# State space scan: the decay matrix is built as exponent(sums spread by float32r plus a mask) on ScalarE

## What is computed

```python
z, xbc, dt = split_cols(h @ w_in, SSM_SPLITS)
xbc = silu(causal_conv4(xbc) + conv_b);  x, B, C = split(xbc)
dt = softplus(dt + dt_bias);  a = dt * -exp(a_log)
cum = cumsum(a)                                # along time, per head
seg = cum[..., :, None] - cum[..., None, :]    # [l, s]
L = exp(where(l >= s, seg, -inf))
y_diag = einsum(C @ B.T, L, x * dt)            # inside a chunk
y_off = C @ state * exp(cum)                   # from the chunk before
y = (y_diag + y_off + d_skip * x) * silu(z);  rmsnorm per group;  @ w_out
```

## Time and profile before

| | |
|---|---|
| median of 3 runs | 2073.43 us (2073.12 to 2076.48) |
| the profiled execution | 2075.21 us, of it the span of the trace 2073.4 us |
| PE busy, share of the span | 1975.6 us, 95% |
| DVE busy | 1725.3 us, 83% |
| ACT busy | 1328.1 us, 64% |
| DMA, mean share of 16 engines | 74% |
| granted TensorE clock, mean | 0.982 of full |
| state space layer's blocks and scan | about 442 to 700 us of the span |
| the scan's 40 steps | about 514 to 667 us |

### The profile page before, as it was taken

How to read it: one execution, slowest core, us unless ns; L and a number is a source line. 1 busy time by engine, 2 the same in 40 slices (tenths; PEclk the granted TensorE clock), 3 DMA queues, 4 the chain that set the end, 5 groups by cost and what they waited for, 6 DMA issues and landing times.

```text
span 2073.4 us, 28446 instructions
## 1 busy us (share of the span) xinstructions
PE 1975.6 (95%) x10316; PEld 1644.3 (79%) x10316; DVE 1725.3 (83%) x2440; ACT 1328.1 (64%) x1977; POOL 0.2 (0%) x4
## 2 busy tenths in 40 slices
PE   6998999989989999999999999999999998999997
PEld 5777889978877788788888878888888876767785
DVE  7798878768776698989989898998989988785764
ACT  4353534355564587788788787888878774554543
POOL 0000000000000000000000000000000000000000
PEclk9999999999999999999999999999999999999999
DMA  9856689846332298999999999999989994672630
GB/s 378 300 170 234 229 301 327 287 142 207 116 111 82 91 382 325 359 334 382 366 351 365 329 368 345 374 352 340 371 325 377 380 354 158 222 247 68 217 122 21
DMA packets 154211, 560.19 MB, mean 270 GB/s; under 512 B 17232, under 2 KB 17488, under 8 KB 153936
## 3 DMA queue, kind: packets, MB, share of 16 engines
q1 hardware_dynamic: 154064, 558.29, 74.1%
HBM read 557.18 MB, written 1.05 MB: 269 GB/s over the span
## 4 chain that ended last, share of the span: by engine, by line
PE 78%; DVE 12%; ACT 5%; issue 3%; DMA 2%; DVEq 0%; SPq 0%; ACTq 0%
PE ps L527 22%; PE ps L529 22%; PE ps L528 22%; PE ps L533 10%; DVE spl L516 3%; PE ps L537 3%; DVE macc L580 2%; ACT sph L504 2%; DMA ring<-in_hyb_w_in 1%; DVE arena L2169 1%; DMA ring<-in_dense_down 1%; ACT arena L771 1%; ACT arena L2135 0%; DVE hL L884 0%; ACT ps L890 0%
## 5 line engine op out<-in xcount | busy, mean ns | idle before, releaser
L504 ACT ACTIVATE sph<-ring 128x1024 fp32r<-128x1024 f32 x906 | 949.2, 1059 | 517.0 <-PE ps L529 332.8
L516 DVE TENSOR_TENSOR spl<-ring,sph 128x1024 fp32r<-128x1024 f32 x906 | 1078.2, 1219 | 241.5 <-ACT sph L504 229.0
L527 PE MATMUL ps<-sph,hH 128*128 128x512 f32 (+1 forms) x1296 | 522.6, 403 | 1.4 <-DVE hL L884 1.3
L529 PE MATMUL ps<-sph,hL 128*128 128x512 f32 (+1 forms) x1296 | 507.8, 392 | 0.0
L528 PE MATMUL ps<-spl,hH 128*128 128x512 f32 (+1 forms) x1296 | 506.9, 391 | 0.0
L529 PEld LDWEIGHTS ps<-sph,hL 128*128 128x128 f32 x1296 | 245.5, 189 | 52.6
L527 PEld LDWEIGHTS ps<-sph,hH 128*128 128x128 f32 x1296 | 246.4, 190 | 51.3 <-issue 3.8
L528 PEld LDWEIGHTS ps<-spl,hH 128*128 128x128 f32 x1296 | 246.4, 190 | 48.4 <-issue 1.0
L527 PE MATMUL ps<-sph,rH 128*128 128x512 f32 x664 | 269.1, 405 | 5.9 <-ACT arena L3123 2.3
L529 PE MATMUL ps<-sph,rL 128*128 128x512 f32 x664 | 259.9, 391 | 0.0
L528 PE MATMUL ps<-spl,rH 128*128 128x512 f32 x664 | 259.4, 391 | 0.0
(11 more groups left out here) (317 smaller groups left out, 1754.4 us busy)
## 6 DMA issues: line engine op xcount, KB each, us to landing
ring<-in_moe_gu SPq DMA_DIRECT2D x448, 512.0 KB, 5.4
ring<-in_moe_down SPq DMA_DIRECT2D x224, 512.0 KB, 5.3
ring<-in_mod SPq DMA_DIRECT2D x144, 512.0 KB, 5.0
ring<-in_w_in SPq DMA_DIRECT2D x64, 512.0 KB, 4.5
ring<-in_dense_gu SPq DMA_DIRECT2D x44, 512.0 KB, 5.3
ring<-in_ssm_w_in SPq DMA_DIRECT2D x40, 512.0 KB, 4.2
ring<-in_dense_down SPq DMA_DIRECT2D x22, 512.0 KB, 5.4
ring<-in_hyb_w_in SPq DMA_DIRECT2D x20, 512.0 KB, 5.9
```

The source lines that it names most:

```text
L504: a.activation(k.high[m % SPLITS][:, 0:w], raw[:, 0:w], ACT.Copy).then_inc(k.S.half_rounded, 1)
L516: v.tensor_tensor(k.low[m % SPLITS][:, 0:w], raw[:, 0:w], k.high[m % SPLITS][:, 0:w], ALU.subtract).then_inc(*k.tick(k.S.half_split, f"hal ...
L527: pe.matmul(out, a[0], b[0], start=start, stop=False, skip_group_check=True)
L529: return pe.matmul(out, a[1], b[0], start=False, stop=stop, skip_group_check=True)
```

## The change

- **The exponent moves and is cut.** At r = 0 and r = 1 ACT reads the bank itself: four exponents of 128 columns with the negated own sum as bias (`M.less`), 64 in all. The 64 DVE instructions at L2280 and the 8 exponents of 1024 columns at r = 2 are gone. Banks with sums are now freed by ACT (`raised{r}`); DVE's product at r = 3 waits for `raised1`.
- **The mask** is a product: the identity by a matrix `past` (0 on and above the diagonal of the stored matrix, -1e30 elsewhere), in float32r, 512 columns, opens each bank.
- **The sums** come from `cum`, turned once per time tile by PE, split into a high part (ACT) and a low part (DVE) in 64 rows of the old `dtw3` tile; a 0/1 column of `pick`, spread over 128 columns, picks both rows of a head. These products are float32r too, one per head, 128 columns.
- **Set up once**, in the dt part: four small DVE writes (zeros, `pick`, `eye`, `past`), the negated sums, the low part; one ACT copy; two transposes on PE.
- The arena grows, two tiles are added, and a scratch area for dynamic DMA is asked for at 1024 bytes.

```diff
@@ time_tensor
     yield
+    bank = banks.take(pe, "cumT", "dt.low")
+    pe.wait_ge(*when("dt.sums"))
+    for t in range(NT):
+        last = turn(pe, k, bank[0:32, t * 128:(t + 1) * 128], M.cum[:, t, :])
+    last.then_inc(*tick(S.dt_tensor, "dt.turned"))
+    yield
@@ time_scalar
+    a.wait_ge(*when("dt.turned"))
+    a.activation(M.cumT[0:32, :], k.banks[k.bank_of.get("cumT", 0)][0:32, 0:T], ACT.Copy).then_inc(*tick(S.dt_scalar, "dt.high"))
+    yield
@@ time_vector
     v.tensor_tensor(M.dte, M.dte, M.dtb[:, 0, :], ALU.mult).then_inc(*tick(S.dt_vector, "dt.weights"))
+    v.memset(M.cumT[64:128, :].bitcast(F32), 0.0).then_inc(*tick(S.dt_vector, "dt.low"))
+    v.tensor_copy(M.pick, k.caus_spare[:, 32:64]).then_inc(*tick(S.dt_vector, "dt.low"))
+    v.tensor_copy(M.eye, k.C["ident"]).then_inc(*tick(S.dt_vector, "dt.low"))
+    v.tensor_scalar(M.past, k.C["triu"], 1.0, -NEG, ALU.subtract, ALU.mult).then_inc(*tick(S.dt_vector, "dt.low"))
+    v.tensor_scalar(M.less, M.cum, -1.0, None, ALU.mult).then_inc(*tick(S.dt_vector, "dt.less"))
+    yield
+    v.wait_ge(*when("dt.high"))
+    v.tensor_tensor(M.cumT[32:64, :], k.banks[k.bank_of.get("cumT", 0)][0:32, 0:T], M.cumT[0:32, :], ALU.subtract).then_inc(*tick(S.dt_vector, "dt.low"))
@@ scan_tensor
         if i is not None and r < 2:
-            bank = banks.take(pe, f"ssd{i}.run{r}", f"ssd{i}.arg{r}")
-            pe.wait_ge(*when("dt.a"))
+            bank = banks.take(pe, f"ssd{i}.run{r}", f"ssd{i}.raised{r}")
+            pe.wait_ge(*when("dt.low"))
+            mm(pe, bank[:, :].rearrange("p (n t) -> p n t", n=4), M.eye, M.past.unsqueeze(1).broadcast_to([128, 4, 128]), True, False)
             for n in range(4):
                 h = 8 * (i // 2) + 4 * r + n
-                last = mm(pe, bank[:, n * 128:(n + 1) * 128], M.a[:, i % 2, h:h + 1].broadcast_to([128, 128]), k.C["triu"])
+                last = mm(pe, bank[:, n * 128:(n + 1) * 128], M.pick[:, h:h + 1].broadcast_to([128, 128]), M.cumT[:, i % 2 * 128:(i % 2 + 1) * 128],
+                          False, n == 3)
@@ scan_scalar
-        if i is not None and r == 2:
-            a.wait_ge(*when(f"ssd{i}.arg1"))
-            a.activation(M.Mt[i % 2], M.Mt[i % 2], ACT.Exp).then_inc(*tick(S.ssd_raised, f"ssd{i}.raised"))
+        if i is not None and r < 2:
+            t, bank = i % 2, k.banks[k.bank_of.get(f"ssd{i}.run{r}", 0)]
+            if r == 0:
+                a.wait_ge(*when("dt.less"))
+                if i >= 2:
+                    a.wait_ge(*when(f"ssd{i - 2}.summed"))
+            a.wait_ge(*when(f"ssd{i}.ran{r}"))
+            for n in range(4):
+                h = 8 * (i // 2) + 4 * r + n
+                a.activation(M.Mt[t][:, 4 * r + n, :], bank[:, n * 128:(n + 1) * 128], ACT.Exp,
+                             bias=M.less[:, t, h:h + 1]).then_inc(*tick(S.ssd_raised, f"ssd{i}.raised{r}"))
@@ scan_vector
-        if i is not None and r < 2:
-            bank = k.banks[k.bank_of.get(f"ssd{i}.run{r}", 0)]
-            if r == 0 and i >= 2:
-                v.wait_ge(*when(f"ssd{i - 2}.summed"))
-            v.wait_ge(*when(f"ssd{i}.ran{r}"))
-            for n in range(4):
-                h = 8 * (i // 2) + 4 * r + n
-                v.tensor_scalar(Mt[:, 4 * r + n, :], bank[:, n * 128:(n + 1) * 128], M.cum[:, t, h:h + 1], 0.0, ALU.subtract,
-                                ALU.min).then_inc(*tick(S.ssd_decayed, f"ssd{i}.arg{r}"))
@@
         if i is not None and r == 3:
-            v.wait_ge(*when(f"ssd{i}.raised"))
+            v.wait_ge(*when(f"ssd{i}.raised1"))
```

More of the change, by code:

```diff
@@ L32 @@
 NI = EXPERT_TILES // 2
-ARENA = 16008
+ARENA = 17000
 INV_2PI = 1.0 / (2.0 * math.pi)
@@ L212, in __init__ @@
         self.arena = sb("arena", [128, ARENA])
+        self.eye, self.past = sb("eye", [128, 128], F32R), sb("past", [128, 128], F32R)
         self.banks = [ctx.enter_context(nc.psum_tensor(f"ps{i}", [128, 512], F32)) for i in range(8)]
@@ L334, in __init__ @@
         self.diag = A.get(NT, 128)
+        shared = k.dtw3.rearrange("p a n -> p (a n)")
+        self.cumT, self.pick = shared[:, 0:T], shared[:, T:T + 32]
+        self.eye, self.past = k.eye[:, :], k.past[:, :]
+        self.less = A.get(NT, 32)
         self.ss, self.rr, self.t8 = A.get(8), A.get(8), A.get(8)
@@ L3417, in constants @@
     c[:, at:at + 30] = p[:, None] % 32 == np.arange(30)[None, :]
+    at = CL["caus"][0] + 160
+    c[:, at:at + 32] = (p[:, None] < 64) & (p[:, None] % 32 == np.arange(32)[None, :])
     put("iota", np.broadcast_to(np.arange(8), (128, 8)))
@@ L3510 @@
     from concourse.bass_utils import run_bass_kernel_spmd as _run
-    nc = _bacc.Bacc("TRN2", target_bir_lowering=False, num_devices=1)
+    nc = _bacc.Bacc("TRN2", target_bir_lowering=False, num_devices=1, dynamic_dma_scratch_size=1024)
     laid = layout(inputs)
```

2 lines of the change are left out of this document (1 added, 1 removed).

## The result

The changed kernel takes 2081.0 us (median of 20 runs, 2078.3 to 2087.6), the kernel before, run beside it, 2075.1 us (20 runs, 2067.1 to 2080.3). The ratio is 1.0034, with a 95% interval of 1.0024 to 1.0044: +7.1 us, with +5.0 to +9.1 as its bounds. (The two medians alone are 5.9 us apart. The profiled execution took 2083.3 us, its span is 2081.5. The forecast was +2.5 us, with "the same" and "slower" at equal chances; the measured time lies inside the range of 2067 to 2082, and the change is outside what counted as the same, and 2.8 times the forecast.

What follows compares the result with a forecast made beforehand. PE was taken to set the pace in the scan, DVE in the dt part. Terms 1.2 - 0.9 - 3.4 + 5.6 = +2.5 us gave a median of 2076.0 us, with 2067 to 2082 as the 8-in-10 range.

Steps and rivals of the forecast that it cites:

- Part 1: Setup in the dt part: six added DVE instructions are paid in full because DVE sets the pace there, +1.2 us.
- Part 2: PE's sums in the scan: a group falls from 0.89 to 0.67 us, counting -0.9 us by itself.
- Rival C: PE's sums: narrow float32r products as slow as f32, 0.22 us instead of 0.11; 2079 to 2083 us, chance 0.09.
- Part 3: Scan: DVE gives up 17.9 us of work, shortening PE's waits for masked products, Silu and norms, -3.4 us.
- The 0.5 at step 4: Item 0's masked product: the exponent no longer stands ahead of ACT's rounding at step 3, -0.5 us.
- Part 4: ACT in the scan: new exponents 0.25 us each, work up 8 us; 23 table loads, ten more, 12.8 us.
- Part 5: Places where ACT is late for PE: steps 1 (+1.3), 9 and 10 (+2.3), 17 and 18 (+1.8), item 7 (+0.2); +5.6 us.
- rival B: ACT becomes the bound: exponents cost 0.56 us, half clock may follow new PE waits; middle 2080.5 us, chance 0.18.
- A: Rival: ACT never late in a way that counts, DVE's relief shows; 2066.6 to 2071.8 us, chance 0.31.
- D: Rival: setup not ready before the scan, PE stands at step 0; no time of its own, 0.02 with others.

Runs made afterwards that it cites:

- e2: The kernel before plus the change's setup and new PE sums; subtract-and-min stay on DVE, the exponent on ACT as before; ratio 1.0001.
- e1: The kernel before plus only the change's setup in the dt part, decay matrix made as before; ratio 0.9989.
- e9: e1 plus four unused 128-column exponents on ACT at steps 0 and 1 of each item, old exponent cut to 8 columns; ratio 1.0030.
- e8: The changed kernel with DVE work put back at the old places, 80 instructions of 112 columns, results unused; ratio 1.0072.
- e17: The changed kernel, unchanged, measured again in a later series; 2080.4 us, ratio to the kernel before 1.0037.
- e10: The changed kernel with the four square roots of the norms moved from ACT to DVE; ratio to the kernel before 1.0046.
- e7: The changed kernel with its 64 exponents replaced by identity, so without most table loads; decay matrix not raised; ratio 0.9971.
- e14: The changed kernel with both groups' sums and all eight exponents of an item at step 2; ratio to the kernel before 1.0025.
- e3: The kernel before plus a one-column exponent on ACT at steps 0 and 1 of each item, adding table loads; ratio 0.9975.
- e13: The changed kernel with both groups' sums of an item at step 1 and all eight exponents at step 2; ratio 1.0132.
- e12: The changed kernel with the setup's identity and mask written ahead of DVE's wait for dt's product; ratio 1.0031.
- e15: The changed kernel with both groups' sums and all eight exponents of an item at step 1; ratio 1.0074.

## Why the prediction was wrong

- **Part 1, the setup (+1.2): right.** Five of the six instructions took 0.18 to 0.27 us, the low part 0.41, and the dt part is 0.6 to 1.8 us longer at equal clock. DVE, from the trace of after:

```profile
464.01 0.27 DVE L2101 MEMSET dtw<- 64x256 f32 x1
464.31 0.18 DVE L2102 CAST dtw<-cst 128x32 fp32r<-128x32 f32 x1
...
464.68 0.19 DVE L2105 TENSOR_SCALAR arena<-arena 128x64 f32<-128x64 f32 x1
...
468.66 0.41 DVE L2108 TENSOR_TENSOR dtw<-ps,dtw 32x256 fp32r<-32x256 f32 x1
```

- **Part 2, the sums (-0.9): right.** 0.63 us a group instead of my 0.67, narrow products at my 0.11. e2's scan is 1.0 us shorter than e1's. Rival C is out.
- **Part 3, DVE's relief (-3.4): there, and put too high.** Step by step after is shorter at step 4 (6.20 to 5.70 us), step 7 (4.97 to 4.28) and step 14 (9.39 to 8.63, with the same loss by clock): 2.0 us. The gains forecast at the norms g = 1 and g = 2 (0.4 and 0.3) didn't come: steps 22 and 23 take 8.37 us before and 8.38 after, steps 30 and 31 take 5.90 and 5.90. The 0.5 at step 4 isn't DVE's: e9, with all of DVE's work, has it too (5.70), so 1.5 are left for DVE. e8 gives 4.5 to 5.5 us of scan for the relief, of which 3.4 to 5.1 half clock, and the ratios 7.9 give or take 4, so its size with the clock in it stays open. The waits that I listed moved less than I wrote (the norms 9.2 to 8.5, not to 7.6; the masked product 3.0 up to 4.1).
- **Part 4, ACT's work: right.** 23 loads, 0.25 us per exponent (1.14 for four in one row, overlap included).
- **Part 5, the late places (+5.6): the step that failed.** The places were right and so was the order in them, but they cost 8.7 us in the profiled execution and 7.7 in e17. Steps 0 and 1: 3.1 instead of 1.3, of it 1.5 by the half clock behind the wait; e10, without it, has 1.6. Steps 8 to 10: 2.2 in e17 against 2.3, and 3.2 in the profiled execution, which has a stretch at half clock there. Steps 16 to 18: 2.4 instead of 1.8, with PE's wait for the bank of the state's product (1.4 us), which is emptied by the move that now stands behind the exponents. So two things were mis-sized. The larger: the price of a stretch at half clock behind a wait stood in rival B, not in the term (2.5 us in the first execution, 1.5 in e17). The smaller: I had followed the Silu through ACT's order, and not the banks that the same instructions free. The 31.4 us that ACT waits for PE, which the prediction set against this, are those of one line; ahead of z ACT waited 9.2 us before and 0.9 after, so there its slack was used up.
- **The balance.** 7.7 to 8.7 in place of 5.6, and 2.0 in place of 3.4, make the sum +6.0 to +7.0. Two stretches at half clock stand outside all my terms: one less at steps 28 and 29 (1.6 us) and one more behind the scan (copies 156 to 158 take 29.20 us before, 29.96 and 29.97 after). That gives some +5.2 to +6.2, inside the measured +5.0 to +9.1; what remains to +7.1 can't be told from nothing.
- **Rivals.** B was nearest: its mechanism of new waits with half clock behind them happened at step 1 in both executions of after, but with exponents at 0.25 us, not its 0.56. A's relief was there in part, and A's case of ACT in time is nearest to e7 (0.9971, 6 us under before), which however also lost loads that before has. D is out.
- **The table loads.** 20 loads less were worth 13 us (e7), ten less some 2 us (e14, intervals overlapping), six less nothing (e10), ten more nothing in the whole (e3), though 4.0 us at the three places. Here a load cost something where PE waits behind it, and nothing that shows elsewhere; e13, which has the ten loads less by moving the reader, cost 20 us more than after. Behind the 1.28 us of a load next to nothing is seen: the root starts 577.22 - (575.93 + 1.28) = 0.01 us after its load, and in after the exponents start 519.94 - (518.64 + 1.28) = 0.02 us after theirs.

What stays open: the 0.25% by which e3 came out under before; whether holding a bank of sums costs something in after (e8 against e9); how much of the half clock is caused by the waits; and with it the true size of DVE's relief. Luck alone it isn't: in the scan, before and e1 have their four stretches at the same steps (14, 22 and 23, 28 and 29, 38 and 39), and after, e17 and e12 share four (1, 14, 22 and 23, 38 and 39) and differ in a fifth (step 8, none, step 10).

## What to carry to other kernels

Moving work to the engine with the lower busy share didn't pay here, because that engine serves in a fixed order things that the bound engine waits for. Before such a move list, for each step, all that stands behind the moved instruction, the copies that free banks as well as the results, and look how long the engine waits just ahead of each of them, not in sum. Keep the producer and the reader of a bank in the same step; a bank held for one step more (e13) cost 18 us of scan against after and 20 against e14, far more than ten table loads. It isn't enough by itself: e15 has both in one step and lost 8 us against after. Where the bound engine gets a new wait of a few us, put the half clock behind it into the term itself: here it came with seven of nine waits of 1.9 to 3.3 us at step 1, with 1.7 us recorded in five of them and 3.4 in two.

## What the runs showed of the hardware

- Float32r products of 128 columns with weights of their own follow each other in 0.11 us (after, L538; the second of each four comes after 0.06), at the same pace as those of 32 and 64 columns before.
- ACT reads 128 columns from a bank with a bias of its own per row every 0.25 us (after, L2284: four in a row take 1.14 us, one takes 0.37).
- A table load takes 1.28 us, and the next activation starts 0.01 to 0.02 us behind it (before and after, at 12 of the 13 loads of before's scan and all 23 of after's; behind the other one, that of z in before, ACT waits 1.7 us for PE).
- The same program loses different amounts to half clock from one execution to the next: after lost 6.8 us of it from copy 100 to 122 in the first profiled execution and 1.7 in e17 (94.3 and 91.6 us). A difference of 2 us in such a stage between two single traces says nothing until runs with the same loss are compared. Taking the recorded loss off is too much: there 5.1 us more of it made the stage 2.7 us longer. In the scan a stretch recorded as 1.7 us made its step 1.5 to 1.6 us longer, the program being the same up to there (step 1, after and e10: 9.04 and 7.56; step 8, after and e17: 8.10 and 6.53).
- Where the stretches at half clock fall on the same steps, two executions of the same scan agree step by step within 0.1 us (before and e1, 157.54 and 157.64 in all).
